# Decoding two attention groups earlier, weights of two tiles in one transfer, and kept halves and split stores at the end

## The reference

```python
hp = rms_norm(yp, g_norm)
qd, kd, vd, gd, qw, kw, vw, gw, qm, gm = split_projection(hp, w_in)   # 2048 x 7168
od = diff_attn_prompt(qd, kd, vd, lam, slopes_diff)      # 4 heads, two softmaxes each
ow = dilated_prompt(qw, kw, vw, slopes_dil)              # 4 heads
mk, mv = memory_kv(mem_prompt, g_mem_norm, w_mem_kv)     # 256 memory tokens, 2048 x 1024
om = memory_attn(qm, mk, mv)
yp = yp + gated_merge(od, gd, ow, gw, om, gm, ..., w_out)  # 2048 x 2048
# the same for the 8 samples, against caches:
od = diff_attn_sample(qd, kd, vd, cache_k_diff, cache_v_diff, page_table, ...)  # 1024 past keys
ow = dilated_sample(qw, kw, vw, cache_k_win, cache_v_win, ...)
om = memory_attn(qm, cache_mem_k, cache_mem_v)
y_prompt, y_sample = rms_norm(yp, g_final), rms_norm(ys, g_final)
```

## Time and profile before

| | |
|---|---|
| median of 3 runs | 1053.77 us |
| profiled execution | 1054.8 us, its span 1053.0 us |
| PE busy | 1004.2 us, 95% |
| DVE busy | 735.9 us, 70% |
| ACT busy | 450.7 us, 43% |
| DMA | 205.42 MB, mean 195 GB/s |

### The profile page before, as it was taken

One profiled execution on the slowest core, in us unless ns is written; L12 is line 12 of the kernel. 1 busy time (PEld: TensorE's weight loads), 2 busy tenths in 40 slices (PEclk: granted clock), 3 DMA queues, 4 the chain that ended last, 5 costly groups with the idle time before them and its releaser, 6 DMA issues. The chain is left out here.

```text
span 1053.0 us, 24106 instructions
## 1 busy us (share of the span) xinstructions
PE 1004.2 (95%) x8078; PEld 980.1 (93%) x8078; DVE 735.9 (70%) x2711; ACT 450.7 (43%) x1183; POOL 53.1 (5%) x124
## 2 busy tenths in 40 slices
PE   6999999999999999999999998989999998999993
PEld 6999999999998999989999998978999998999993
DVE  5682222777788878678787766648775698888874
ACT  5763222223332333343434552313566456555562
POOL 0200000000000000000000000000000200000002
PEclk9999999999999999999999999999999999999997
DMA  9763333899876998767767658989765326332354
GB/s 293 241 197 103 96 91 98 264 266 295 255 243 205 273 251 245 240 191 228 232 197 217 208 171 272 241 219 302 215 211 150 106 77 205 113 108 81 96 146 162
DMA packets 258265, 205.42 MB, mean 195 GB/s; under 512 B 12640, under 2 KB 211926, under 8 KB 256982
## 3 DMA queue, kind: packets, MB, share of 16 engines
q1 hardware_dynamic: 257966, 203.81, 64.5%
q10 hardware_dynamic: 176, 0.07, 0.0%
HBM read 192.07 MB, written 11.76 MB: 194 GB/s over the span
## 5 line engine op out<-in xcount | busy, mean ns | idle before, releaser
L1060 PE MATMUL z<-act_hi,w_hi 128*128 128x260 f32 (+2 forms) x2048 | 448.1, 292 | 8.6 <-DVE w_lo L1629 8.1
L1060 PE MATMUL z<-act_hi,w_lo 128*128 128x260 f32 (+2 forms) x2048 | 428.7, 283 | 0.0
L1060 PE MATMUL z<-act_lo,w_hi 128*128 128x260 f32 (+2 forms) x2048 | 428.0, 283 | 0.0
L1060 PEld LDWEIGHTS z<-act_hi,w_hi 128*128 128x128 f32 x2048 | 324.8, 189 | 14.3 <-DVE w_lo L1629 6.6
L1060 PEld LDWEIGHTS z<-act_lo,w_hi 128*128 128x128 f32 x2048 | 323.4, 189 | 0.0
L1060 PEld LDWEIGHTS z<-act_hi,w_lo 128*128 128x128 f32 x2048 | 322.9, 189 | 0.0
L1629 DVE TENSOR_TENSOR w_lo<-w_raw,w_hi 128x512 fp32r<-128x512 f32 x316 | 216.3, 687 | 126.9 <-ACT w_hi L1311 126.3
L1311 ACT ACTIVATE w_hi<-w_raw 128x512 fp32r<-128x512 f32 x316 | 195.1, 626 | 220.2 <-PE z L1060 176.6
L1819 DVE CUSTOM_DVE_ANT_0 pages<-pages,q_bc 128x128 f32<-128x128 f32 x640 | 144.4, 285 | 48.9 <-DMA pages<-in_cache_k_win_dram 20.1
L1848 DVE SCALAR_TENSOR_TENSOR v_acc<-pages,dec_a,v_acc 128x256 f32<-128x256 f32 x224 | 94.0, 478 | 1.6 <-DMA pages<-in_cache_v_diff_dram 1.5
L1433 ACT ACTIVATE probs<-probs,st_n 128x128 f32<-128x128 f32 (+3 forms) x48 | 26.8, 558 | 87.5 <-DVE st_n L1758 87.1
(11 more groups left out here) (224 smaller groups left out, 1074.3 us busy)
## 6 DMA issues: line engine op xcount, KB each, us to landing
w_raw<-in_w_in_dram SPq DMA_DIRECT2D x224, 256.0 KB, 4.3
pages<-in_cache_k_diff_dram SPq DMA_DIRECT2D x128, 256.0 KB, 4.4
pages<-in_cache_v_diff_dram SPq DMA_DIRECT2D x128, 256.0 KB, 3.5
w_raw<-in_w_out_dram SPq DMA_DIRECT2D x72, 256.0 KB, 2.9
w_raw<-in_w_mem_kv_dram SPq DMA_DIRECT2D x32, 256.0 KB, 6.5
cat<-in_x_prompt_dram SPq DMA_DIRECT2D x8, 1024.0 KB, 7.3
q_bc<-q_rows_dram SPq DMA_DIRECT2D x32, 256.0 KB, 6.6
pages<-in_cache_mem_k_dram SPq DMA_DIRECT2D x16, 256.0 KB, 6.6
```

Of the source, the lines that this page charges most:

```text
L1060: last = nc.tensor.matmul(zb[:, bank, 0:b - a], lhs[:, w], rhs[:, kt, a:b], start=(kt == 0 and m == 0), stop=(kt == KT - 1 and m == 2))
```

## The change

It has four parts.

1. **Earlier decoding.** The query rows of group 0 (the first four query tiles) are stored by themselves after the fourth tile, and its key units start in slot 52, not 68. The end stays at slot 241, so 320 units are spread over 190 slots instead of 174.
2. **Loads of two tiles.** For all input tiles but mk0, mk1, vw and gw, one DMA brings a quarter of two neighbouring tiles (512 KB in pieces of 1 KB, not 256 KB in pieces of 512 bytes) into two raw slots. It is due one slot after both are free, not four. The first vw and gw tiles' loads are due early as well.
3. **Kept halves.** Both halves of the last two output tiles' weights are kept in an idle part of the arena, so that part 2 needs no loads and no splits (8 fewer of each).
4. **The end.** The norms of blocks 2 and 3 are one slot earlier; y is stored in halves of 512 KB; y_sample in one DMA, not 16, behind blocks 2 and 3; the last square of block 1 is on DVE beside ACT's of block 0; 1/D and epsilon go into the squares, so that GpSimd has one instruction for 1/rms; block 1's second half is scaled on DVE, and ACT issues the stores of block 1 itself.

```diff
+FIRST_KEPT = START[UNIT_OF[AT["y", KT - TWICE, 1]]]
+N_SPLITS = FIRST_AGAIN
+SIDE_BY_SIDE = ("mk", "mv", "qd", "kd", "vd", "gd", "qm", "qw", "kw", "gm")
 def raw_loads():
+        if k is None and loaded_together(tiles[0]):
+            ...
+            for r in range(4):
+                at, slot, a, b = min((max(x[0], y[0]), x[1], x[2], y[2]) for x in free for y in free
+                                     if x[1] % 2 == 0 and y[1] == x[1] + 1)
+                ...
+                q = first + 4 + r
+                for i in range(2):
+                    gone.append((q - AHEAD, slot + i, ("lo", q + 1)))
+                loads.append((n, r, slot, used[slot], event, at + 1))
 ...
-            loads.append((n, r, slot, used[slot], event, at + (1 if first >= IN_END else AHEAD + 1)))
+            soon = first >= IN_END or TILES[n] in (("vw", 0, 0), ("gw", 0, 0))
+            loads.append((n, r, slot, used[slot], event, at + (1 if soon else AHEAD + 1)))
 ...
-                for k in range(4):
-                    put(s + 4 + k, "norm", (2 + k // 2, k % 2))
-                for k, later in enumerate((2, 3, 6, 7)):
+                for k in range(2 * (NBLK - HEAD)):
+                    put(s + 3 + 2 * k // (4 - HEAD), "norm", (HEAD + k // 2, k % 2))
+                for k, later in enumerate((2, 3, 6, 8)):
 ...
-    put(DONE[AT["qd", 3, 1]] + 1, "qrows", 0)
+    put(DONE[AT["qd", 1, 1]] + 1, "qrows", 0)
+    put(DONE[AT["qd", 3, 1]] + 1, "qrows", 1)
-    first, end = DONE[AT["qd", 3, 1]] + 4, DONE[AT["gw", 3, 0]] + 2
+    first, end = DONE[AT["qd", 1, 1]] + 4, DONE[AT["gw", 3, 0]] + 2
 ...
+            def halves(q):
+                if q >= FIRST_KEPT:
+                    return (w_kept[:, (q - FIRST_KEPT) % (4 * TWICE), i, :] for i in range(2))
+                return w_hi[:, q % SPLIT_RING, :], w_lo[:, q % SPLIT_RING, :]
 ...
-                        for kt in range(KT):
-                            sp.dma_start(y_sample.rearrange("b a f -> (b a) f")[:, kt * P:(kt + 1) * P], ...
+                        sp.dma_start(y_sample.rearrange("b a (k p) -> k (b a) p", p=P), rows[:, 1, :]).then_inc(s_yout, 16)
 ...
-            norm_last(1)
+            norm_last(1, 0)
+            for half in range(2):
+                cols = slice(half * D_MODEL // 2, (half + 1) * D_MODEL // 2)
+                act.wait_ge(s_ydone[1] if half else s_ylast, 1)
+                act.dma_start(y_prompt.rearrange("a (t p) f -> (a t) p f", p=P)[1][:, cols], nat[:, 1, cols]).then_inc(s_yout, 16)
 ...
+            def square_last():
+                nc.vector.tensor_tensor_reduce(part[:, 0, 0:P], nat[:, 1, e * P:(e + 1) * P], nat[:, 1, e * P:(e + 1) * P],
+                                               1.0 / D_MODEL, 0.0, ALU.mult, ALU.add, y_ss[:, 1, e:e + 1]).then_inc(s_ysq, 1)
 ...
             mean(1)
             times_g(N_TILES - 1)
-            norm_last(0)
+            norm_last(0, 0)
+            norm_last(0, 1)
+            norm_last(1, 1)
 ...
-                link(nc.gpsimd.tensor_scalar(y_sum[:, i:j], y_r[:, i:j], 1.0 / D_MODEL, EPS, ALU.mult, ALU.add))
```

More of the change, by code:

```diff
@@ L50 @@
 WIN_RING = 8
+FIRST_LOADS = WIN_RING - 1
 SPLIT_RING = 4
@@ L181, in raw_loads @@
         first, k = START[u], PAIR_AT.get(u)
+        if first >= FIRST_AGAIN:
+            continue
+        if k is None and loaded_together(tiles[0]):
+            n = tiles[0]
+            second = (TILES[n][2] if TILES[n][0][1] == "d" else TILES[n][1]) % 2
+            if second:
+                continue
+            gone = []
+            for r in range(4):
+                at, slot, a, b = min((max(x[0], y[0]), x[1], x[2], y[2]) for x in free for y in free
+                                     if x[1] % 2 == 0 and y[1] == x[1] + 1)
+                free = [x for x in free if x[1] not in (slot, slot + 1)]
+                event = max((e for e in (a, b) if e is not None), default=None)
+                of_op[first + r] = of_op[first + 4 + r] = len(loads)
+                q = first + 4 + r
+                for i in range(2):
+                    gone.append((q - AHEAD, slot + i, ("lo", q + 1)))
+                    used[slot + i] += 1
+                used[slot + 1] -= 1
+                loads.append((n, r, slot, used[slot], event, at + 1))
+            free += gone
+            continue
         sources = [(None, r) for r in range(4)] if k is None else RAW_ORDER
@@ L743, in wait_raw, with tile_raw @@
             return w_raw[:, slot, :]
+        def tile_raw(engine, q):
+            load = LOAD_OF_OP[q]
+            n, _, slot, _, _, _ = LOADS[load]
+            raw = wait_raw(engine, load)
+            if n >= FIRST_OUT or not loaded_together(n):
+                return raw.rearrange("p (k f) -> p k f", k=4)
+            second = UNITS_OF_TILES[OPS[q][0]][0] - n
+            both = w_raw[:, slot:slot + 2, :].rearrange("p a f -> p (a f)").rearrange("p (k f) -> p k f", k=4)
+            return both[:, :, second * P:(second + 1) * P]
         def wait_weights(engine, q):
             if q in LOAD_OF_OP:
-                return wait_raw(engine, LOAD_OF_OP[q])
+                return tile_raw(engine, q)
             u, o = OPS[q]
@@ L800, in weights @@
                     sp.wait_ge(s_lo if kind == "lo" else s_sum, value)
-                dst = w_raw[:, slot, :].rearrange("p (k f) -> p k f", k=4)
+                if n < FIRST_OUT and loaded_together(n):
+                    dst = w_raw[:, slot:slot + 2, :].rearrange("p a f -> p (a f)").rearrange("p (k f) -> p k f", k=4)
+                else:
+                    dst = w_raw[:, slot, :].rearrange("p (k f) -> p k f", k=4)
                 sp.dma_start(dst, raw_source(n, r)).then_inc(s_raw[slot], 16)
@@ L861, in _ @@
                 weights(i)
-            for q in range(4, WIN_RING - 1):
+            for q in range(4, FIRST_LOADS):
                 weights(q)
@@ L969, in _ @@
                 sp.wait_ge(s_kvout[i], 16 * 12)
-            for i in range(3):
+            for i in range(4):
                 sp.wait_ge(s_qdram[i], 16)
@@ L1053, in quarter @@
                     pe.wait_ge(s_clo, 4 * r + 4)
-                hi, lo = w_hi[:, q % SPLIT_RING, :], w_lo[:, q % SPLIT_RING, :]
+                hi, lo = halves(q)
                 for j in range(4):
```

115 lines of the change are left out of this document (70 added, 45 removed).

## The result

The changed kernel takes **1037.92 us** (median, 1035.88 to 1041.05), the kernel before in the same series 1054.69 us (1052.11 to 1057.22): ratio 0.9844 [0.9808, 0.988]. The profiled execution of the changed kernel is the longest of its four, 1041.05 us with a span of 1039.2, so its trace shows a gain of 13.8 us, 3 us less than the medians do.

What follows compares the result with a forecast made beforehand. PE, busy 1004.2 of 1053.0 us, was taken as the bound, leaving its idle time and lower clock to gain. Tail −4.9, middle −5.0, softmax −0.5 and costs +0.4 made −10.0: 1044.3 us, range 1038.5 to 1050.5.

Steps and rivals of the forecast that it cites:

- Tail: After PE's last transpose: scalings begin earlier and fewer bytes are left to store, −4.9 us, bounds −2.5 to −5.5.
- The middle: MEMORY and WINDOW key phases of the input projection: waits and low clock partly go, −5.0 us, bounds 0 to −9.8.
- the weights' earlier place: WINDOW phase: weights for slots up to 215 are in the ring before query rows crowd the DMA engines; no separate size.
- the nine slots for eight: MEMORY's 16 key units spread over slots 186 to 194, before 190 to 197; counted within the −5.0 us.
- The path of the stall: MEMORY and WINDOW keys: full DMA engines land weights late, DVE gets `w_hi` late, PE uses up three slots of lead.
- The lower bound −9.8: Most the middle could gain: 8.1 us of PE's `w_lo` waits plus 1.7 us of low clock.
- Softmax: Slots 233 to 600 as named there: fewer units per slot, some decode softmax waits go; −0.5 us, bounds −3 to +3.
- Start: Memory stage: paired loads go out later where DMA engines are full; +0.3 us, bounds 0 to +2.
- 4.0 us behind the residual loads stay: Paired output tiles: PE's four `w_lo` waits behind 4 MB of residual loads, 4.0 us, were to remain.
- Rate of the stores in 4 KB pieces: Last stores: 4 KB pieces instead of 8 KB move near the better end of 284 to 414 GB/s, costing +0.3 us.
- The burst rival: Slots 52 to 207, 20 paired groups: 512 KB loads land late and stop PE; likelier 1061 us, slower given 0.06.
- all of it goes: Rival: the middle's 9.8 us and 3.6 us of softmax waits all go, 1036.4 us, chance 0.12.

Runs made afterwards that it cites:

- the thinner front alone: Against the version with parts 1 and 2 undone (1050.4 us), decoding starts at slot 52 but all units from slot 175 on keep their old places: 1046.76 us.
- whole rows: Query rows of one sample side by side in DRAM, broadcasts in 2 KB pieces: 1037.07 us with late decoding, 1029.77 with early, both single loads and new end.

## Why the prediction was off, step by step

- **Tail, −4.9.** Right: −4.8 in the profiled pair, −5.0 with the end alone. Its steps came as told. From PE's last transpose to the scalings it takes 2.1 us instead of 3.2: 0.41 by the addition, which now waits for PE and not for a scaling, 0.42 by the squares side by side and 0.28 by GpSimd, where 0.45, 0.4 and 0.3 were forecast. The version with the end alone contains the kept halves, so those were not measured apart.
- **The middle, −5.0, bounds 0 to −9.8. This is the step that failed.** Measured: −8.5 us between quarters 186 and 240 in the profiled pair, and −10.4 by the early start alone (211.6 to 201.2 us, both with single loads). Wrong was the step from equal bytes to "some of the stall should stay", and with it the half that was taken. The bytes did stay, but the stall did not follow them: new places for the units behind slot 175 took 8.7 us, faster landing broadcasts 13.3 by median. The credit given to the weights' earlier place was empty. The forecast gave the nine slots for eight a sentence and no number; the keys' places are the term, though spreading cannot be all of it, since WINDOW's keys were not spread.
- **The path of the stall was wrong too.** The forecast had weights landing late, "DVE got its `w_hi` late" and PE out of lead. The queue was rightly named, and not VectorE's load. But VectorE stood 24.3 us for key pages from 640 to 715 us and 1.1 for `w_hi`; the weights of all five stalled quarters were split in time on ScalarE. That agrees with the paired and early loads, which brought weights sooner and gave nothing.
- **The lower bound −9.8 was no bound.** It summed the waits for `w_lo` and one clock interval. All idle time of PE between quarters 186 and 240 was 13.3 us before and 6.0 after (4.5 with single loads), since small waits by other names (`cat`, `k_nat`, `probs`) stood in the same stretch.
- **Softmax, −0.5, bounds −3 to +3.** The second term that was sized too small: −3.4 between quarters 80 and 186 in the profiled pair, −3.6 by median with the thinner front alone. The waits for `o_nat` (2.1) and `dc` (1.5) went nearly whole; 0.6 us for `dc` is left in another place.
- **Start, +0.3, bounds 0 to +2.** The mechanism named was the right one and its size far off: +2.9 by quarter 20, undone by loading the memory tiles singly (−1.8 by median). It shows as the wait of 2.2 us for `r_diag` (0.6 with single loads) and a clock of 0.97 over 20 to 75 us where the version with single loads has 1.00. The three slots of lead counted on did not cover ACT's waits of 7.9 us.
- **4.0 us behind the residual loads stay.** Right, to the tenth; the burst of 4 MB was about half of its cause.
- **Rate of the stores in 4 KB pieces.** 350 GB/s at a share of 0.88, so 398 at full share, close to the 414 of 8 KB pieces: the +0.3 was fair.
- **The burst rival** did not come: PE has no `w_lo` wait in the input projection before quarter 217.
- **The rival "all of it goes"**, put at 0.12, forecast 1036.4 us and came nearest. Its reason was half right: it let the waits go whole, which they nearly did, and had no cost of pairing in it.

In the profiled pair the sum reads +3.0 − 3.4 − 8.5 − 0.1 − 4.8 = −13.8, against −10.0 forecast: the middle and the softmax gave 6.4 us more than taken, the start cost 2.7 more. The medians are another 3 us apart, and no trace shows where, since the changed kernel was profiled in its slowest run.

## What to carry to other kernels

When an engine starves, follow its wait through the list of the engine that is late. Here ScalarE's 30 us of waits for weights were the loudest row, and none of PE's five stalls hung on them; `w_lo` stood behind key units whose pages had not landed. Then ask of each transfer in a full queue how long it takes to land, and not only how many bytes it moves, and look first at the small-looking ones that are read many times: laying out 128 rows of scratch in another order was worth as much as the whole replanning. When a change thins or moves a load that runs close to what the queue passes, do not scale the stall with the bytes: most of it went here while the bytes stayed, and small waits by other names went with it. And before a credit goes to the visible part of a diff, find the version in which only that part is undone.

## What the runs showed of the hardware

- The time of a broadcast from DRAM depended on how its source row is cut. 512 pieces of 512 bytes against 128 of 2 KB for the same 256 KB: 6.6 against 4.6 us to landing, and −13.3 us for the kernel by this alone. The Trainium skill, DMA: Bandwidth & Descriptors, Specifications, puts the line rate at 512 bytes and above. It speaks of the rate, and there these two traces do not contradict it: the DMA engines were busy for 670 us in both. Other stretches do disagree: 284 GB/s at full share for 512-byte loads against 398 and 414 for stores in 4 and 8 KB pieces. None of these rates shows the time to landing, which counted here. For weights 1 KB pieces gave no more than 0.9 us over 512 bytes, within the runs' scatter.
- A DMA share of 0.9 or more says nothing by itself of a stall: from 640 to 715 us it was 0.89 with 9.1 us of idle PE, and 0.94 with 2.3 when the broadcasts landed sooner.
- The versions with whole rows, and the one without the broadcasts of MEMORY and WINDOW, scattered by 0.4 to 1.5 us over five runs. The other versions scattered by 1.2 to 6.4, the kernel before by 5.9 over nine. It does not follow the stalls alone: the early start with single loads has one wait for `w_lo` left in the input projection and scattered by 5.2.
